# Row products in steps of 256 columns instead of 512 in a chain of five transformer-like half-blocks

## The reference, cut to what matters

```
stage 0: x += g_a * rms(moba_attention(h))      8 heads of 128, causal, 256 keys
stage 1: x += g_f * rms(swiglu(h))              h @ (1024 x 5632), silu(g)*u, @ (2816 x 1024)
stage 2: x += g_a * rms(diff_attention(h))      8 heads, two half-heads subtracted
stage 3: x += g_f * rms(swiglu(h))
stage 4: x += g_a * rms(conformer(h))           h @ (1024 x 2048), gate, 31-tap conv, layernorm, silu, @ (1024 x 1024)
stage 5: x += g_f * rms(conv_ffn(h))            h @ (1024 x 5632), 3-tap conv, silu(g)*u, @ (2816 x 1024)
h = rms_norm(x) * (1 + sc) + sh                 sc, sh, g: silu(c) @ (1024 x 6144) + bias, per block
```

## Time and profile before

| | |
|---|---|
| median of 3 runs | 984.08 us |
| profiled execution | 984.03 us |
| its span, first to last instruction | 982.2 us |
| PE busy | 947.5 us (96%), 6806 matmuls |
| PEld busy | 868.6 us (88%), 6806 loads |
| DVE busy | 820.6 us (84%) |
| ACT busy | 544.3 us (55%) |
| POOL busy | 78.0 us (8%) |
| granted TensorE clock, mean over the span | 0.993 |
| DMA | 234.08 MB, mean 238 GB/s |

### The profile page before, as it was taken

One profiled execution on the slowest core, in us unless ns is written; L12 is line 12 of the kernel. 1 busy time (PEld: TensorE's weight loads), 2 busy tenths in 40 slices (PEclk: granted clock), 3 DMA queues, 4 the chain that ended last, 5 costly groups with the idle time before them and its releaser, 6 DMA issues. The chain is left out here.

```text
span 982.2 us, 19019 instructions
## 1 busy us (share of the span) xinstructions
PE 947.5 (96%) x6806; PEld 868.6 (88%) x6806; DVE 820.6 (84%) x1217; ACT 544.3 (55%) x1023; POOL 78.0 (8%) x111
## 2 busy tenths in 40 slices
PE   4899999999999999998999999999999999999997
PEld 3899988999999888996999999989997899999996
DVE  4869988898888778777888888889998979988885
ACT  3465546454444566555554444459998555555552
POOL 2100002000000011111300000002240000000000
PEclk9899999999999999999999999999999999999999
DMA  9999983999999965652599999986340549766641
GB/s 347 328 329 349 336 278 97 349 350 343 303 333 322 279 193 162 183 174 84 166 348 359 321 322 317 318 267 173 87 129 1 181 134 301 220 196 192 190 127 43
DMA packets 240770, 234.08 MB, mean 238 GB/s; under 512 B 7497, under 2 KB 208970, under 8 KB 240714
## 3 DMA queue, kind: packets, MB, share of 16 engines
q1 hardware_dynamic: 237824, 226.52, 73.7%
q0 software_dynamic: 1616, 5.32, 1.7%
q10 hardware_dynamic: 1274, 1.52, 0.5%
HBM read 232.27 MB, written 1.06 MB: 238 GB/s over the span
## 5 line engine op out<-in xcount | busy, mean ns | idle before, releaser
L537 PE MATMUL work<-h_hi,whi_a 128*128 128x256 f32 x1360 | 379.0, 279 | 2.8 <-DVE h_lo L1412 2.8
L537 PE MATMUL work<-h_lo,whi_a 128*128 128x256 f32 x1360 | 377.4, 277 | 0.0
L537 PE MATMUL work<-h_hi,wlo_a 128*128 128x256 f32 x1360 | 377.3, 277 | 0.0
L1351 DVE TENSOR_TENSOR wlo_a<-raw,whi_a 128x1024 fp32r<-128x1024 f32 x180 | 218.6, 1223 | 52.2 <-ACT whi_a L1009 51.8
L537 PEld LDWEIGHTS work<-h_hi,whi_a 128*128 128x128 f32 x1360 | 256.3, 188 | 6.4 <-issue 2.9
L537 PEld LDWEIGHTS work<-h_lo,whi_a 128*128 128x128 f32 x1360 | 256.8, 189 | 2.7
L537 PEld LDWEIGHTS work<-h_hi,wlo_a 128*128 128x128 f32 x1360 | 256.4, 189 | 0.0
L1009 ACT ACTIVATE whi_a<-raw 128x1024 fp32r<-128x1024 f32 x180 | 187.9, 1054 | 61.1 <-PE work L537 38.3
L1361 DVE SCALAR_TENSOR_TENSOR acc<-ada_raw,csil,acc 128x1024 f32 (+1 forms) x128 | 163.5, 1279 | 7.2 <-DMA ada_raw<-in_ada_w 5.6
L1009 ACT ACTIVATE whi_b<-raw 128x1024 fp32r<-128x1024 f32 x106 | 110.7, 1055 | 81.4 <-DMA raw<-in_ffn_w_out 42.8
L1351 DVE TENSOR_TENSOR wlo_b<-raw,whi_b 128x1024 fp32r<-128x1024 f32 x106 | 128.5, 1219 | 8.8 <-ACT whi_b L1009 8.6
(11 more groups left out here) (228 smaller groups left out, 1395.6 us busy)
## 6 DMA issues: line engine op xcount, KB each, us to landing
ada_raw<-in_ada_w SPq DMA_DIRECT2D x88, 512.0 KB, 6.4
raw<-in_ffn_w_in SPq DMA_DIRECT2D x88, 512.0 KB, 7.9
ada_raw<-in_mod_w SPq DMA_DIRECT2D x48, 512.0 KB, 6.8
raw<-in_ffn_w_out SPq DMA_DIRECT2D x44, 512.0 KB, 6.2
raw<-in_f_up_w SPq DMA_DIRECT2D x44, 512.0 KB, 4.3
raw<-in_moba_w_qkv SPq DMA_DIRECT2D x24, 512.0 KB, 8.4
raw<-in_diff_w_qkv SPq DMA_DIRECT2D x24, 512.0 KB, 8.0
raw<-in_a_pw_w SPq DMA_DIRECT2D x24, 512.0 KB, 7.4
```

Source lines behind the costliest of these rows:

```text
L537: mm = pe.matmul(dst, w[u][:, ws], h[:, k, :], start=(k == 0 and m == 0), stop=(k == KT - 1 and m == 2))
L1351: dve.tensor_tensor(wlo[u], raw[:, u, :], whi[u].bitcast(F32), ALU.subtract).then_inc(lo[u], 1)
```

## The change

A new helper `half_bank` issues one matmul of 256 columns into half of a bank of `Y`: half `g` of bank `bank`, from the 256 columns of the unit that belong to it. `row_tile` and `row_quarter` call it for g = 0 and g = 1 where they issued one matmul of 512 columns. The stationary operand of the two is the same and is loaded for each. `start` is given with the first half of a bank alone and `stop` with the second. The order of parts, tiles and banks stays, and so do the semaphores, which follow the last matmul of a group as before.

```diff
+            def half_bank(bank, g, a, w, start, stop):
+
+                at = (bank % 2) * HALF + g * S
+                return pe.matmul(Y[:, bank, g * S:(g + 1) * S], a, w[:, at:at + S], start=(start and g == 0),
+                                 stop=(stop and g == 1))
+
             def row_tile(a_h, a_l, u, n, t, first=False, end=False):
 
                 pe.wait_ge(lo[u], n + 1)
...
                 if end:
                     for f in range(2):
                         for m, (a, w) in enumerate(parts):
-                            mm = pe.matmul(Y[:, 2 * t + f, :], a[:, ts], w[u][:, f * 512:(f + 1) * 512],
-                                           start=False, stop=(m == 2))
+                            for g in range(2):
+                                mm = half_bank(2 * t + f, g, a[:, ts], w[u], False, m == 2)
                         mm.then_inc(*((used[u], 1) if t and f else (y_done, 1)))
                 else:
                     for m, (a, w) in enumerate(parts):
                         for f in range(2):
-                            mm = pe.matmul(Y[:, 2 * t + f, :], a[:, ts], w[u][:, f * 512:(f + 1) * 512],
-                                           start=(first and m == 0), stop=False)
+                            for g in range(2):
+                                mm = half_bank(2 * t + f, g, a[:, ts], w[u], first and m == 0, False)
                     if t == TT - 1:
                         mm.then_inc(used[u], 1)
 
             def row_quarter(a_h, a_l, u, n, q, first=False):
 
-                t, f = q // 2, q % 2
+                t = q // 2
                 pe.wait_ge(lo[u], n + 1)
                 for m, (a, w) in enumerate(((a_h, whi), (a_h, wlo), (a_l, whi))):
-                    mm = pe.matmul(Y[:, q, :], a[:, t * P:(t + 1) * P], w[u][:, f * 512:(f + 1) * 512],
-                                   start=(first and m == 0), stop=False)
+                    for g in range(2):
+                        half_bank(q, g, a[:, t * P:(t + 1) * P], w[u], first and m == 0, False)
```

## The result

The changed kernel takes 994.36 us (median of 4 runs, 993.88 to 995.53) against 984.14 us before: ratio 1.0099, 95% interval 1.0086 to 1.0112. It is slower by 10.2 us, 1%. The direction was forecast, and the range of 976.5 to 995 holds the time, but the size was not forecast: 10.2 us against 4.6. Of all executions that follow, one (1847 us, of the kernel with the last product wide, whose other three took 994 to 997) is a slow run and is left out of its median and ratio.

The account below looks back on a forecast made before the run. TensorE was taken to set the time from about 35 us on. Half the row products short and half long gave -1.8 us, half of 64 pairs long +6.4, sum +4.6, so 988.7 us, range 976.5 to 995.

Parts of the forecast that it names:

- Bound by TensorE, costs read as distances between starts: From about 35 us on TensorE sets the time, so a matmul's start-to-start distance goes straight into the total.
- Number: 1080 matmuls become 2160: The 90 row products of 12 matmuls of 512 columns become 2160 of 256, with 1080 more weight loads.
- A row product, -0.07 or +0.03 us: A split row product takes 2.72 us in the short step or 2.82 in the long, against 2.79 now.
- A pair behind a row product, +0.20 us when long: A pair of column products behind a row product takes 5.65 us if long against 5.45; all 64 cost 12.8 us.
- half of the 64 pairs long, 32 x 0.20 = +6.4 us: Half the pairs directly behind row products go long, +6.4 us; half was a choice between 0 and +12.8 us.
- The 6 of 6 at the seam from values to pair: In attention, pairs behind short-step value products went long at 6 of 6 places, suggesting more than half the pairs long.
- the 1 of 2 out of a long stream: Behind long-step value products, one pair went short and one stayed long, suggesting more than half the pairs long.
- The doubt about the seam out of `ab`: Whether row product to pair behaves like values (stationary `h`) to pair was open, drawing the estimate back to half.
- Rival A: Row products at 2.72 us and pairs at 5.45, all short: 977.2 us, or 980.5 if loads limit; chance 0.30.
- B: Long step in the row products alone, pairs unchanged: +2.7 us, 986.8 us; chance 0.11.
- C: Row products and pairs all long, with no fall back: +15.5 us, 999.6 us; chance 0.07.
- D: Row products at the mean of both steps, -1.6 us, few pairs long, effects cancel: 982.5 to 985.5 us; chance 0.10.

Follow-up runs that it names:

- last product wide: Only the last of a row product's 12 products left 512 columns wide, the other 11 split; against the kernel before, 994.94 us, ratio 1.0110.
- Tail of 2: First and last two of a row product's 12 products left 512 columns wide, 9 split; against the kernel before, 981.08 us, ratio 0.9977.

## Why the prediction was right and wrong, point by point

- **Bound by TensorE, costs read as distances between starts.** Right. PE's waits hardly changed, and of the 9.9 us between the two profiled spans 8.4 lie in the three feed-forward stages, where PE is full.
- **Number: 1080 matmuls become 2160.** Right, 7886 matmuls against 6806.
- **A row product, -0.07 or +0.03 us.** The direction was right and the short step came, but -0.07 was too much: 2.79 to 2.74 us in the feed-forward stages. I took 24 short distances and left out the settling behind the seam, which the trace of before showed for the other seam at 168.47 to 168.59. That a split product against `ab` costs what one against `h` does came true.
- **A pair behind a row product, +0.20 us when long.** Right in mechanism and in size, 5.45 to 5.65 us.
- **The step that failed: "half of the 64 pairs long, 32 x 0.20 = +6.4 us", with half of the row products long.** All 64 were long: from start to start these pairs took 12.1 us more in the trace of after than in that of before. All row products together took 3.4 us less, where the sum has 1.8: nearly all of those in the feed-forward stages were short, most of those in attention long. I took the state at a seam for something to be averaged. Out of a short stream it follows a fixed rule, and in a loop that repeats it settles into one cycle: the experiments have 0, about half or all of the pairs long, by what stands at the seams. The 6 of 6 at the seam from values to pair was the rule and not a tendency (55 of 55 in the later traces); the 1 of 2 out of a long stream was no rule and stayed none (15 of 33). The doubt about the seam out of `ab`, which drew my number back to half, was unfounded: out of short it behaves as the seam out of `h`. With what the trace has, the same sum is 12.1 - 3.4 = +8.7 us of the 9.9 between the profiled spans. Another 0.9 us lie ahead of the first pair, which starts at 35.0 us before and at 35.9 after; over all twelve traces this start varies from 34.7 to 36.1 us, both for kernels whose pairs stay short and for those whose pairs go long, so I do not charge it to the change. The last 0.3 us are spread over the other products.
- **Rival A, short everywhere, 977.2 us.** Did not come by the change. Tail of 2 is its mechanism made to happen, at 981.08 us: three products stay wide and the pairs behind the values of attention stay long.
- **Rivals B, C, D.** B had row products long and pairs as before, the reverse of what came. C's "long stays long" came at the four pairs behind a long row product, but its row products did not stay long: behind a long pair a split row product went short at all 247 places of the traces. D's cancelling did not come.
- **The pages.** The row product got cheaper by splitting, 2.79 to 2.74 us, where the fixed part per matmul of the Trainium skill ("TensorE: Matmul & The Clock Gate", section "Back-to-back issue gap") would have made it dearer; its +2.7 us have the right sign for the total by another cause. The section gives that formula for an isolated matmul and says that in a stream of loads and matmuls both set the spacing, so it need not hold for this stream. The other sentence that the prediction took from the Trainium skill (same page, section "Step-by-step: what each phase is for"), that a load takes no read bandwidth from the running matmul, does not rule out a long step behind a seam. The prediction's " contradict" does not follow, and no run here separates the load from the stream.

## What to carry to other kernels

Measure a dense stream of matmuls by the distance between starts, for each kind of product, and compare it at all its places: two values of the same instruction (113 and 118 ns here) are a state that the stream before it has set, and an edit can move it in code that it does not touch. A cheaper form of one product is worth only what is left after its neighbours; look at a seam of the same two kinds elsewhere in the trace, and where it always does the same, take that as a rule in a loop and not as a chance. Here the gain came by leaving the products at the seams as they were: the first and the last two of twelve.

## What the runs showed of the hardware that was not expected

- fp32r matmuls of 256 columns with a load of 128 columns each settle at 113.3 ns or at 117.7 ns from start to start and stay there through a pair or a row product that nothing interrupts, at a granted clock of 1.00 (the 2.4 GHz level) in both cases. The duration of one is 276 or 281 ns.
- A 512-column matmul costs 232.5 ns in a stream of its kind, 5.9 ns more than two of 256 in the short step.
- The step of a stream depends on the stream before it. Behind a short one, a swap of roles between weights and activations gives a long one (215 of 215 from row product to pair, 55 of 55 from values to pair, 44 of 44 from pair to row product). Without a swap an odd number of 512-wide matmuls between gives a long one (28 of 28) and an even number a short one (24 of 24). Two or more of them before the swap to a pair give a short pair (276 of 276). Behind a long stream the outcome is mixed at most places.
- The state is not bound to a change of the PSUM tensor, since the seam from values to pair stays within `work`, nor to which weight buffer moved last. What in the engine or the memory holds it stays open; it was not tried to move operands to other addresses.
